# Input projections of a hybrid decoder step as three rounded matmul passes, with weight tiles split ahead by ScalarE and VectorE

## What is computed

```python
hn = rmsnorm(x, norm_mix)
proj = hn @ w_in                      # 1024 x 9248
z, xbc, dt_raw, uv, gates = jnp.split(proj, [...])
...                                   # causal conv + silu of xbc, softplus of dt
y_ssd, new_ssm = ssd_chunked(xs, dt, a_log, b_ssm, c_ssm, ssm_init)
y_ssd = rmsnorm((y_ssd + d_skip * xs) * silu(z), gnorm_w)
u, v = jnp.split(gelu(uv), 2, axis=-1)
y_mlp = u * (W_s @ layernorm(v) + b_s)
merged = sigmoid(g_ssd) * (y_ssd @ w_branch_ssd) + sigmoid(g_mlp) * (y_mlp @ w_branch_mlp)
h = x + merged @ w_out
h = h + moe(rmsnorm(h))               # top 4 of 32 experts, float32 weights
```

## Time and profile before

| | |
|---|---|
| median of 3 runs | 1642.72 us (1641.45 to 1643.35) |
| profiled execution, its own time | 1642.57 us |
| its span | 1640.8 us |
| start to the first projection | 25.4 us |
| first 19 projection tiles and `mix`, until pair 0 | 100.3 us |
| the 16 pairs | 330.8 us |
| branches until the first expert weights are used up | 200.3 us |
| from there to the end | 984.0 us |

### The profile page before, as it was taken

The page is one execution under the profiler, slowest core; times in us unless marked ns, Lnnn a source line. Parts: engine busy times, 40 slices in busy tenths (PEclk is TensorE's granted clock), DMA queues, the critical chain, the costliest instruction groups (busy, mean ns, idle before and its releaser), DMA issues.

```text
span 1640.8 us, 20898 instructions
## 1 busy us (share of the span) xinstructions
PE 1515.8 (92%) x8031; PEld 825.4 (50%) x8032; DVE 547.0 (33%) x1269; ACT 321.8 (20%) x573; POOL 179.8 (11%) x288
## 2 busy tenths in 40 slices
PE   5999999999899999999989999997899899999986
PEld 3676666666699965434443443443243334334432
DVE  1365565654474424322221221311132222212213
ACT  2243344433253205100100100100011001001002
POOL 3002222322266000000000000000000000000000
PEclk9999999999799999999999999999999999999998
DMA  8442344444254454999999999999799999999993
GB/s 258 132 135 79 106 132 116 122 132 136 72 153 136 150 209 163 405 428 427 428 429 428 429 428 429 429 429 427 296 427 428 429 429 429 429 428 429 428 428 159
DMA packets 123032, 495.77 MB, mean 302 GB/s; under 512 B 6865, under 2 KB 94973, under 8 KB 97549
## 3 DMA queue, kind: packets, MB, share of 16 engines
q1 hardware_dynamic: 85216, 471.74, 70.8%
q10 hardware_dynamic: 35888, 18.88, 4.2%
q0 software_dynamic: 1872, 4.39, 0.9%
HBM read 483.65 MB, written 11.34 MB: 302 GB/s over the span
## 4 chain that ended last, share of the span: by engine, by line
PE 64%; DMA 25%; DVE 5%; issue 3%; ACT 2%; SPq 1%; POOL 1%; ACTq 0%; DVEq 0%; POOLq 0%
DMA ring_b<-in_w_gu 24%; PE bank L1278 16%; PE bank L801 13%; PE bank L1331 10%; PE bank L1117 7%; PE bank L1231 3%; PE bank L786 2%; PE bank L1026 2%; PE bank L1132 2%; PE bank L1037 2%; PE bank L1387 1%; DVE arena L1979 1%; PE bank L1267 1%; DVE arena L2063 1%; DVE arena L1977 1%
## 5 line engine op out<-in xcount | busy, mean ns | idle before, releaser
L1278 PE MATMUL bank<-ring_b,xe 128*64 128x512 f32 x1280 | 354.9, 620 | 42.4 <-DMA ring_b<-in_w_gu 42.4
L801 PE MATMUL bank<-arena,ring 128*128 128x320 f32 (+1 forms) x912 | 266.2, 442 | 0.5 <-ACT arena L1463 0.5
L1278 PEld LDWEIGHTS bank<-ring_b,xe 128*64 128x64 f32 x1280 | 116.4, 142 | 265.2 <-issue 264.8
L1278 PE MATMUL bank<-ring,xe 128*64 128x512 f32 x768 | 226.0, 594 | 5.2 <-DMA ring<-in_w_gu 5.0
L1331 PE MATMUL bank<-ring,actT 128*64 128x512 f32 x768 | 227.8, 596 | 0.0
L801 PEld LDWEIGHTS bank<-arena,ring 128*128 128x128 f32 (+1 forms) x912 | 167.7, 191 | 64.2 <-issue 4.6
L2289 DVE TENSOR_SCALAR swi<-bank 128x256 f32<-128x256 f32 x64 | 27.2, 424 | 341.9 <-PE bank L1278 336.8
L1451 ACT ACTIVATE swi<-swi 128x256 f32<-128x256 f32 x66 | 27.4, 416 | 569.5 <-DVE swi L2289 569.5
L1117 PE MATMUL bank<-rounded,rounded 128*128 128x320 f32 x608 | 134.2, 310 | 1.7 <-DVE ring_r L2111 1.7
L1331 PE MATMUL bank<-ring_b,actT 128*64 128x512 f32 x256 | 113.5, 596 | 4.3 <-ACT actT L1791 4.3
L1278 PEld LDWEIGHTS bank<-ring,xe 128*64 128x64 f32 x768 | 75.0, 137 | 76.6 <-issue 76.6
(11 more groups left out here) (346 smaller groups left out, 1732.4 us busy)
## 6 DMA issues: line engine op xcount, KB each, us to landing
ring_b<-in_w_gu SPq DMA_DIRECT2D x83, 2048.0 KB, 16.9
ring<-in_w_down SPq DMA_DIRECT2D x50, 2048.0 KB, 18.7
ring<-in_w_gu SPq DMA_DIRECT2D x49, 2048.0 KB, 16.8
ring<-in_w_in SPq DMA_DIRECT2D x32, 1024.0 KB, 5.3
ring_b<-in_w_down SPq DMA_DIRECT2D x16, 2048.0 KB, 14.6
arena<-in_state_ssm ACTq DMA_DIRECT2D x16, 512.0 KB, 5.3
out<-arena ACTq DMA_DIRECT2D x16, 512.0 KB, 3.8
ring<-in_w_branch_ssd SPq DMA_DIRECT2D x8, 1024.0 KB, 5.3
```

The lines of the kernel that those rows point to most:

```text
L801: mm = pe.matmul(bank[q % 2][0:cols, 0:T], w, hnT[:, k, :], start=(k == 0), stop=(k == KD - 1))
L1278: mm = pe.matmul(bank[q][side(h), :], xe[:, j, side(h)], moe_slot(2 * i + h)[:, 2 * FF * k + 512 * q:2 * FF * k + 512 * q + 512], start=Fa ...
```

## The change

All projection tiles are now made like the branches, in three passes of rounded values. What it does:

- ScalarE writes the high part of the normalised, transposed activations straight from PSUM (`hn_hi`), VectorE the low part (`hn_lo`); `hnT` is gone, and so is its split beside pair 14 and 15.
- Each weight tile (128 columns) is split on its own: `split_tile(q)` on ScalarE rounds tile q into one of two slots for high parts, `split_tile(q)` on VectorE subtracts in place. It is done for tile q + 4 right after tile q is read (ScalarE) or convolved (VectorE). The first three are split before the activations are.
- The mixer's ring has four slots; slots 4 and 5 of `ring_r` hold the high parts. The expert ring is laid out so that four chunks (`EARLY`) can be loaded before the mixer is done.
- dt is the first chunk and tile; its softplus and running sums are made beside the v tiles, so the table-based functions stand in another order on ScalarE.
- The tiles of a group are spread over its pairs as 3, 3, 2, 2 in place of 3, 2, 3, 2, in another order.
- `csout` is kept small: the rows of a group are stored at once, by four GpSimd DMAs per group in place of two in all.

```diff
-MOE_RING = 6
-EARLY = 3
+MOE_RING = 6
+MIX_RING = 4
+DT_COLS = KD * H + P - H
+EARLY = 4
...
-    out = [("v", m) for m in range(4)]
-    out += [("dt", 0), ("z", 0), ("z", 1), ("x", 0), ("x", 1), ("bc", 0)]
+    out = [("dt", 0)] + [("v", m) for m in range(4)]
+    out += [("z", 0), ("z", 1), ("x", 0), ("x", 1), ("bc", 0)]
     for g in range(1, G):
-        out += [("x", 2 * g), ("x", 2 * g + 1), ("bc", g), ("z", 2 * g), ("z", 2 * g + 1)]
+        out += [("x", 2 * g), ("z", 2 * g), ("x", 2 * g + 1), ("bc", g), ("z", 2 * g + 1)]
...
+SPLIT = PROJ + [((kind, 0), t) for kind in ("gs", "gm") for t in range(2)]
...
-    return [[("conv", c), ("conv", c + 1), ("conv", c + 2)],
-            [("conv", c + 3), ("conv", c + 4)],
-            [("conv", c + 5), ("z", z), ("z", z + 1)],
+    return [[("conv", c), ("conv", c + 1), ("z", z)],
+            [("z", z + 1), ("conv", c + 2), ("conv", c + 3)],
+            [("conv", c + 4), ("conv", c + 5)],
             [("z", z + 2), ("z", z + 3)]][jj]
...
             for n, c in enumerate(CHUNKS):
-                if n >= RING:
-                    if n - RING < N_PROJ:
-                        sp.wait_ge(S["proj_ready"], tiles_through(n - RING))
+                if n >= MIX_RING:
+                    if n - MIX_RING < N_PROJ:
+                        sp.wait_ge(S["proj_ready"], tiles_through(n - MIX_RING))
...
+            def store_rows(g):
+                pool.wait_ge(S["cs_ready"], 2 * g + 2)
+                ...
+                    pool.dma_start(dst[:, x], csout[c0 + r0:c0 + r1, 0:512]).then_inc(cs_out, 16)
+                    pool.dma_start(...).then_inc(cs_out, 16)
...
-                if j == 4 * G - 4:
-                    pool.wait_ge(S["cs_ready"], 2 * G)
-                    pool.dma_start(conv_prompt_new[0, 0], csout[0:KEEP, :]).then_inc(cs_out, 16)
-                    ...
+                if j % 4 == 0:
+                    store_rows(j // 4)
...
             def half_tile(q, i):
+                o = bank[q % 2][:, 0:T]
                 if i == 0:
-                    if t == 0:
-                        chunk_ready(pe, c)
+                    pe.wait_ge(S["split_lo"], q + 1)
                     if q >= 2:
                         pe.wait_ge(S["proj_read"], q - 1)
-                for k in range(4 * i, 4 * i + 4):
-                    w = ...
-                    mm = pe.matmul(bank[q % 2][0:cols, 0:T], w, hnT[:, k, :], start=(k == 0), stop=(k == KD - 1))
+                    else:
+                        pe.wait_ge(S["hn_hi_ready"], KD)
+                    for k in range(KD):
+                        pe.matmul(o, w_h[k], hn_hi[:, k, :], start=(k == 0), stop=False)
+                    for k in range(4):
+                        pe.matmul(o, w_l[k], hn_hi[:, k, :], start=False, stop=False)
+                else:
+                    for k in range(4, KD):
+                        pe.matmul(o, w_l[k], hn_hi[:, k, :], start=False, stop=False)
+                    if q == 0:
+                        pe.wait_ge(S["hnT_ready"], KD)
+                    for k in range(KD):
+                        mm = pe.matmul(o, w_h[k], hn_lo[:, k, :], start=False, stop=(k == KD - 1))
...
+            def split_tile(q):                       # ScalarE
+                c, t = SPLIT[q]
+                n = AT[c]
+                if t == 0:
+                    chunk_ready(act, c)
+                if n >= 2:
+                    freed = CHUNKS[n - 2]
+                    act.wait_ge(S["proj_ready"], PROJ.index((freed, t if freed[0] != "dt" else 0)) + 1)
+                w, hi, _ = tile_of(q)
+                act.copy(hi, w).then_inc(S["split_hi"], 1)
+
+            act.wait_ge(S["ident_ready"], 1)
+            for q in range(3):
+                split_tile(q)
             for k in range(KD):
                 act.wait_ge(S["hnT_psum"], k + 1)
-                act.copy(hnT[:, k, :], bank[(0, 1, 6, 7)[k % 4]][:, 0:T]).then_inc(S["hnT_ready"], 1)
+                act.copy(hn_hi[:, k, :], bank[(2, 3, 6, 7)[k % 4]][:, 0:T]).then_inc(S["hn_hi_ready"], 1)
...
                 elif kind == "u":
                     read_u(n)
+                if kind != "gs":
+                    split_tile(tile_no(kind, n) + 4)
...
-                if kind == "hn":
-                    act.wait_ge(cs_out, 32)
...
+                for tile in tiles[-2:]:
+                    if tile == tiles[-1]:
+                        for n in late:
+                            silu(n)
+                        late = []
+                    read_beside(tile)
+                    late += [n for kind, n in (tile,) if kind == "conv"]
...
+            def split_tile(q):                       # VectorE
+                dve.wait_ge(S["split_hi"], q + 1)
+                w, hi, lo = tile_of(q)
+                dve.tensor_tensor(lo, w, hi.bitcast(F32), ALU.subtract).then_inc(S["split_lo"], 1)
+
+            for k in range(KD):
+                if k in (0, 2, 5):
+                    split_tile((0, 2, 5).index(k))
+                dve.wait_ge(S["hn_hi_ready"], k + 1)
+                dve.tensor_tensor(hn_lo[:, k, :], bank[(2, 3, 6, 7)[k % 4]][:, 0:T], hn_hi[:, k, :].bitcast(F32),
+                                  ALU.subtract).then_inc(S["hnT_ready"], 1)
...
+            def convolve_beside(n):
+                convolve(n)
+                split_tile(tile_no("conv", n) + 4)
...
+                if kind != "gs":
+                    split_tile(tile_no(kind, n) + 4)
```

More of the change, by code:

```diff
@@ L110, in sem_of @@
 def sem_of(c):
[L112 to L118, removed]
+    return MIX_RING + c % MOE_RING
 def build(nc, x_prompt, x_sample, state_conv, state_ssm, norm_mix, w_in, conv_w, conv_b, dt_bias, a_log,
@@ L185, in after_r @@
             return place(top[0], *shape, parts=True)
-        hnT = place(0, KD, T)
-        mlpT = after(KD, T)
+        squared = place(0, D)
+        mlpT = place(KD * T, KD, T)
         base = top[0]
@@ L192, in build @@
         vtok = place(base + 4 * T, 3, D)
-        csin = place(base + PAIRS * T, CONV)
-        junk = after(D)
-        nm_row = after(D)
+        nm_row = place(KD * T, D)
+        vw_row = after(D)
         yT = place(base, PAIRS, T)
-        csout = after(CONV)
+        hn_hi = after_r(KD, T)
+        csout = after(DI // G + 2 * N)
         raw = after(2, SPAN + DB * STEP)
@@ L202, in build @@
         xsT = [after(4, T) for _ in range(2)]
-        bcT = [after(2, T)]
+        bcT = [after(2, T) for _ in range(2)]
         off = after(T - P)
-        wb_first = place(base + 13120, SLOT, parts=True)
-        bcT.append(after(2, T))
         cbm = after(T)
@@ L243, in build @@
         assert ssd_top <= tail, ssd_top
-        hn_hi = place(base + PAIRS * T, KD, T, parts=True)
-        mergedT = after(KD, T)
+        mergedT = place(base + PAIRS * T + KD * T, KD, T)
         gate_s = after(2, T)
@@ L480, in build, with high_of, low_of, tile_of @@
         MIX_BANKS = (5, 6, 3, 7)
-        BRANCH = ([("w", 0), ("hn", 0), ("w", 1), ("mlp", 0), ("w", 2)] + [("y", i) for i in range(4)]
+        BRANCH = ([("mlp", 0), ("w", 2)] + [("y", i) for i in range(4)]
                   + [("w", i) for i in range(3, 20)])
         FIRST_BRANCH = AT[("gs", 0)]
+        def high_of(n):
+            return ring_r[:, MIX_RING + n % 2, :].rearrange("p (k n) -> p k n", k=KD)
+        def low_of(n):
+            return ring_r[:, n % MIX_RING, :].rearrange("p (k n) -> p k n", k=KD)
+        def tile_of(q):
+            c, t = SPLIT[q]
+            n = AT[c]
+            if c[0] == "dt":
+                d = slice(0, DT_COLS)
+                return ring[:, n % MIX_RING, d], ring_r[:, MIX_RING + n % 2, d], ring_r[:, n % MIX_RING, d]
+            d = slice(t * P, t * P + P)
+            return wide(n)[:, :, d], high_of(n)[:, :, d], low_of(n)[:, :, d]
         def branch_item(item):
@@ L855, in _ @@
                 turn_v(m - 1)
-            project("dt", 0)
+            project("z", 0)
             turn_v(7)
-            for i in range(4):
+            for i in range(1, 4):
                 project("z", i)
@@ L1555, in _ @@
-            for n in range(2, CG):
-                silu(n - 2)
+                    act.copy(csout[32 * g:32 * g + STATE_ROWS, 512:768], bank[2][0:STATE_ROWS, 0:2 * P]
+                             ).then_inc(S["cs_ready"], 1)
+            for i in range(4):
+                read_z(i)
+                if i == 2:
+                    for c in range(3):
+                        act.wait_ge(S["ln_var"], c + 1)
+                        act.sqrt(small[0:rows(c), 44 + c:45 + c], small[0:rows(c), 40 + c:41 + c]
+                                 ).then_inc(S["ln_std"], 1)
+                split_tile(tile_no("z", i) + 4)
@@ L1557, in _ @@
+            for n in range(CG):
+                if n >= 2:
+                    silu(n - 2)
                 read_conv(n)
+                split_tile(tile_no("conv", n) + 4)
+                if n == 3:
+                    act.wait_ge(S["v_ready"], 3)
```

(8 more changed lines are left out.)

330 lines of the change are left out of this document (157 added, 173 removed).

## The result

The changed kernel takes 1631.72 us (median of 18 runs, 1624.0 to 1639.3), the kernel before 1639.61 on the same chips (18 runs, 1634.2 to 1647.3). The ratio is 0.9948, with a 95% interval of 0.9933 to 0.9964: faster, by 0.5%, or 8.5 us by the ratio (the two medians lie 7.9 apart). The forecast was 38 us. The profiled execution took 1635.9 us, its span is 1634.1, against 1640.8 before: 6.7 less, and its stages say where the rest went.

What follows compares the result with a forecast made beforehand. TensorE's work was taken to bound the mixer, the weight stream the experts. Terms +2.9 - 10.3 - 8.0 - 4.9 - 17.7 = -38.0 us against 1642.57 gave 1604.6, rounded 1605; range 1584 to 1632.

Steps and rivals of the forecast that it cites:

- The bound and the expert stage: TensorE's work bounds the mixer; expert stage stays 984.0 us and shifts whole, its seventh chunk asked for at 619.
- Tile cost: Projection tiles on TensorE: 3.52 us in three passes, where float32 took 4.33; 0.81 us saved a tile.
- The start: Until the first projection: +2.9 us, at 28.3 in place of 25.36, bounds 0 and +6.
- The first 19 tiles: First 19 tiles and `mix`, up to pair 0: -10.3 us, from 15.4 saved less 0.5 and 4.6.
- Pairs 0 to 11 and 12 to 14: Shorter tiles, partly given back in new waits: -8.0 us (bounds -27, +4) and -4.9 us.
- (b): Rival: clock falls behind some new waits, 2 us each, six to sixteen falls, 1616 to 1636 us; chance 0.22.
- (c): Rival: clock falls and stays in two-tile pairs, some 36 us a group, slower, up to 1713 us; chance 0.09.
- windows at 0.50 among the pairs: Sign of being wrong: half the granted clock among the pairs would point to (b) or (c).
- Pair 15: Last pair: -17.7 us, from 33.6 to a two-tile pair of 15.0 plus the last diagonal, 0.9.
- Covered at nothing: Four-slot ring, last out chunk, GpSimd's 16 small stores and split of `mlpT`: 0 us, the last with bound +2.
- The split beside GpSimd: In the pairs, VectorE's splits and GpSimd's reads may exclude each other; left out of the sum, upper bound otherwise.

Runs made afterwards that it cites:

- e7: Changed kernel, reordered: ScalarE's splits, state stores and late Silu behind copies TensorE waits for, VectorE's sample states earlier; 1582.2 us, ratio to kernel before 0.9646.
- e5: Changed kernel plus six unread TensorE passes in every pair, ahead of the wait for the second state copy; 1615.3 us, ratio to kernel before 0.9848.
- e12: Changed kernel with three expert chunks loaded early (`EARLY = 3`) in place of four; 1636.1 us, ratio to kernel before 0.9969.
- e3: Changed kernel with VectorE's split subtractions in the pairs cut to one column; pairs 0 to 14 took 301.8 us, not 318.1; kernel time disturbed.
- e8: e7 with the last split ahead of the pairs made after the mix biases (VectorE) and the last rows (ScalarE); 1584.1 us.

## Why the prediction was right and wrong

**The bound and the expert stage**: right. 983.9 us behind the seventh request, and what the pairs lost or gained came out at the end. The request itself came at 650.2, for 619.

**Tile cost**: right. Useful work in pairs 0 to 14 was 297.2 - 5.3 = 291.9 us before, and is 265.3 - 3.4 = 261.9 in e7. 30.0 us for 38 tiles is 0.79 each; the forecast had 0.81.

**The start**: right, 27.55 for 28.3. ScalarE began the splits of the first v chunk at 20.21, as soon as it had landed, and not at 21.0: that is the difference. They took 1.99 us, and from their end, 22.2, to the first projection it was 5.4, as booked.

**The first 19 tiles**: -11.9 for -10.3. From the last tile's end to pair 0 it was 9.3 us before and is 12.6 now (103.37 to 115.92): 3.2 more, for the 4.6 booked, with a wait of 2.01 in it for a bias behind a split, and a clock of 0.68 from 110 to 120 us, which the forecast did not have.

**Pairs 0 to 11 and 12 to 14**: here it failed. The forecast was 30.8 saved by tiles and 17.9 given back in waits, -12.9. What happened is 30.0 saved, 17.1 given back in waits, and 33.8 lost to the clock: useful work took 295.7 us where e7 has 261.9. -30.0 + 17.1 + 33.8 = +20.9. (e5 makes the loss 31, by another way.)

The waits were right in sum and by the mechanism named: a split at the head of ScalarE's chain, and the copies for which TensorE then waits. In pair 2, a jj of 2, TensorE waited 0.30, 1.04 and 0.71 us at the three places for which 0.6, 1.1 and 1.2 were booked. That the sum came so near is partly luck: the 3.0 us for VectorE's sample states in pairs 4 and 8 and the longest wait, 2.34 in pair 13, were not foreseen, and in part make up for booked waits that came out shorter.

The step that failed is the price of a new wait. The sum took each at its own length and put the clock behind it at nothing; that it might fall was rival (b), given 0.22. The waits booked were 0.6 to 1.3 us, and the trace before had one of 1.18 that left the clock alone and one of 1.54 that did not. A wait of 1.09 was enough. And (b) had a fall end with the next tile, for 2 us; in pair 1 it lasted for 13 us and cost 6. That half of the mechanism stood under (c), where pair 15 before was read rightly: passes between small matmuls didn't bring the clock back. Falls longer than (b)'s and shorter than (c)'s 36 us a group, behind some of the waits only, landed by luck inside (b)'s 1616 to 1636, and with 1631.7 just inside the stated range of 1584 to 1632. The windows at 0.50 among the pairs, named as a sign of being wrong, are there.

**Pair 15**: right, -17.6 for -17.7.

**Covered at nothing**: the ring of four, the out chunk, the small stores and `mlpT` cost nothing: the branches took 0.2 us less than before, and no wait for a load of the mixer appears among the view's waits. `EARLY` was right at zero (e12).

**The split beside GpSimd**: the rule of the Trainium skill ("SBUF — State Buffer", section "Who interferes with whom") was left out of the sum. The traces agree with the rule, and show that GpSimd pays. VectorE's split has a median of 1218 ns in after and a longest of 1789; the 61 take 75.4 us, 1.1 more than 61 medians. But GpSimd's scaling of a pair's output (L696), median 1086 ns before, has 1642 in after, 1129 in e3, without these splits, and 1960 in e7. In pair 3 of e7 it runs from 180.38 for 3.67 us, and two splits, 2.35 us, lie wholly inside (the profile's spans on GpSimd are rough). In the pairs nothing waits for L696, so leaving it out was right: e7 runs at full clock with these instructions at their longest. Cutting the splits on VectorE (e3) gained 16 us in a single profile, of which its waits explain 2; what share of the rest is VectorE's stays open.

## What to carry to other kernels

When an engine's tiles get shorter, what another engine does for it moves onto the path, even where that engine is idle half of the time; work with a late due time (here splits that are wanted four tiles later, stores, a Silu) belongs behind the copy that the fast engine waits for next. Price a new wait of TensorE by what its clock does behind it, not by its length: here 17 us of new waits came with 31 to 34 us lost to the clock. To find out, fill the wait with passes into a spare bank: here that made the kernel faster, and showed that it was the clock.

## What was not expected of the hardware

- A wait of 1.09 us was followed by half the clock, while TensorE was busy without a gap for the next 13 us. In e3 and e12 a wait of 1.10 at the same instruction was not, and of six waits of 1.14 to 1.17 us in e7 and e8 one was. What else decides is open.
- Once at 1.2 GHz, TensorE stayed there through a half tile of 12 passes and the small matmuls around it, and came back in the 24 passes in a row at the pair's end (pair 1, from 157.09).
- 90 passes in pairs 0 to 14 whose result nothing reads, 15.6 us of work in the profile (and six in pair 15), made the kernel 16 us faster (e5).
- Executions differ with the clock. After's 18 spread over 15.3 us, and its longer ones have the lower mean clocks; before's 18, with falls in pairs 1 and 15, spread over 13.1; e7's four over 3.2.
- A VectorE instruction with two inputs in SBUF lengthened one of GpSimd: two splits of 2.35 us in all, inside one that takes 1.08 us alone and took 3.67 there (e7).
